# Sparse and stick-breaking attention on one Trainium2 core: value products cut along the keys instead of along the queries, one PSUM bank per head, each batch fed in two phases

## The chip, the cores and the metric

One kernel on one core of a Trainium2 chip. The metric is the device time of one execution in microseconds (us); lower is better. The engines are named as in the profile: PE is TensorE's matmul side, PEld its weight loads, DVE is VectorE, ACT is ScalarE, POOL is GpSimd, SP issues most of the DMAs.

## The reference, cut to what matters

The kernel computes a two-layer trunk over 2048 tokens. Two of its attention stages are touched. In the first layer it is stick-breaking attention with 8 heads of 64, strictly causal in blocks of 128 queries; in the second it is sparse attention with 16 heads of 64, where keys that were not chosen carry a very negative score in a table that is added. (The kernel multiplies the latents out to keys and values per head beforehand.)

```
# stick-breaking, one block of 128 queries, keys 0..L-1
z = einsum('bqhd,bkhd->bhqk', q, k) * scale
log_keep = where(causal, log_sigmoid(-z), 0)
suffix = cumsum(log_keep, reverse=True) - log_keep
a = where(causal, exp(log_sigmoid(z) + suffix), 0)
out = einsum('bhqk,bkhd->bqhd', a, v)          # the value product
# sparse, one block of 128 queries
s = einsum(q_lat, c_sel) * scale - slope * dist
p = softmax(where(sel_ok, s, -inf))
out = (p @ c_sel) @ w_uv                        # the value product
```

## The kernel before, in words

Both stages, `stick_breaking` (4 pairs of heads) and `sparse_attention` (8 pairs), have the same frame. Queries and keys come in blocks of 128. For one pair of heads, `paired_groups` (L1294) walks the 16 query blocks in the order of `TURNS` (L1290); for a block b the b+1 key blocks are cut into parts of at most four blocks, the last part first. One **group** is one part of one head: m key blocks, 1 to 4. The two heads of a pair alternate, so groups come in twos. A pair of heads has 80 groups, four groups make a **batch** (BATCH = 4); stick-breaking has 320 groups or 80 batches, sparse attention 640 groups or 160 batches. A **turn** is a set of query blocks whose results share one PSUM bank `o_ps`; there are 12 turns to a pair of heads.

What happens to a group, by engine:

- **score** (PE, `PairTiles.score`, L1367): three products in float32r, each with 64 rows (one head's 64 features; the pair's two heads lie in the two halves of the partitions) and a stationary of 128 queries, against up to 512 keys. The output goes to one of four banks (`s_ps` or `z_ps`).
- then in sparse attention **bias** on DVE (L1614, adds the table, takes the maximum) and the exponential on ACT (L1565); in stick-breaking the sigmoid on ACT (`keep`, L1824), the scan on DVE (L1872), the difference on POOL (L1851). In stick-breaking the sigmoid overwrites its bank, so the bank comes free with the scan.
- **turn** (PE, `turn_pair`, L1385): transposes of 64 query rows by 128 keys, stationary the 64x128 piece of the probabilities, moving a 64x64 identity; queries 0..63 of both heads go to bank `t_ps[0]`, queries 64..127 to `t_ps[1]`. The two pieces of a key block alternate between the two halves of the rows.
- **copy out** to `pT` in SBUF (stick-breaking: ACT, L1831; sparse: every fourth DVE, the others ACT, L1553).
- **feed** (PE, `feed_group`, L1396): the value product. Per key block and query half one matmul in plain float32, contraction over all 128 keys, stationary 128 keys x 64 queries, moving the values (64 columns, 65 in sparse attention with a column of ones), into the lower or upper 64 partitions of the turn's bank. The trace shows two instructions for each such matmul.
- at the end of a turn the **drain**: in sparse attention DVE divides (L1639, L1640) and POOL multiplies by the gate (L1590); in stick-breaking DVE multiplies by the gate, once per unit (L1884).

The order on PE is written out. In sparse attention one batch n is: turn(n), score(n+16), score(n+18), turn(n+2), then the four feeds of the batch before. In stick-breaking: turn(n), score(n+8), turn(n+2), score(n+10), then the four feeds of the batch before. Two banks `o_ps` alternate by turn, so the first feed of a turn waits for the drain of the turn before the last (L1523, L1796). DVE in sparse attention: one copy out, two biases, drains of turns that ended two batches earlier, two biases. In stick-breaking: two scans, such drains, two scans. `turn(n)` waits for the probabilities and for the copies of the two groups before; `score(k)` waits until the bank of group k-4 is free. SP loads the next pair's keys, queries, values and gates (`load_values` waits on `fed`).

Of the kernel before, what the change touches and what calls it, by code (L numbers as in the profile page):

```python
# [36 lines left out]
P = 128  # L37
# [1251 lines left out]

TURNS = [[0, 1], [2, 3], *([b] for b in range(NT - 1, 7, -1)), [7, 6], [5, 4]]  # L1290
BLOCKS = [b for turn in TURNS for b in turn]

def paired_groups(pairs):  # L1294

    units, out = [], []
    for j in range(pairs):  # L1300
        for turn, x, b in ((n, x, b) for n, turn in enumerate(TURNS) for x, b in enumerate(turn)):
            both = [Unit(j, hh, b, list(range(b + 1))) for hh in range(2)]
            parts = chunks(b + 1, GB)[::-1]
            for u in both:
                u.ng, u.turn, u.slot = len(parts), j * len(TURNS) + turn, 2 * (b - min(TURNS[turn])) + u.hh
# [89 lines left out]

def feed_group(nc, o_ps, pT, v, g, vc, fed, w=HD):  # L1396

    for x in range(g.m):
        for half in range(2):  # L1400
            x0 = (g.u.hh * g.m + x) * HD
            last = nc.tensor.matmul(o_ps[half * HD:(half + 1) * HD, 0:w], pT[half][:, x0:x0 + HD],  # L1402
                                    v[:, g.u.kbs[g.a + x], vc:vc + w],
                                    start=(g.first and x == 0 and g.u.hh == 0), stop=(g.last and x == g.m - 1),
                                    skip_group_check=True)
    last.then_inc(fed, 1)

def sparse_attention(nc, c, fm, kc, vc, gc, y, scores, ahead, tiles):
# [17 lines left out]
    with Scope(nc) as sc:  # L1427
# [25 lines left out]
        turned = sc.sem("turned")  # L1453
        taken = {"s": sc.sem("taken_s"), "v": sc.sem("taken_v")}
        fed = sc.sem("fed")
        slopes_set = sc.sem("slopes_set")
# [4 lines left out]
        with nc.Block() as block:  # L1461
# [37 lines left out]
            def _(pe):  # L1499
# [18 lines left out]

                def feed(n):
                    g = gs[n]  # L1520
                    u, p = g.u, g.u.j
                    if g.first and u.turn >= 2:
                        pe.wait_ge(drained, u.turn - 1)  # L1523
                    if n % (PER_PAIR) == 0:
                        pe.wait_ge(v_in[p % 2], (p // 2 + 1) * 32)
                        if n == 0:
                            pe.wait_ge(tables_set, 1)
                    if n % 2 == 0:
                        for x in (n, n + 1):
                            pe.wait_ge(taken[who[x]], nth[x])  # L1530
                    x0 = u.slot * SW
                    feed_group(nc, o_ps[u.turn % 2][:, x0:x0 + SW], [pT[(n - u.hh + x) % TB] for x in range(2)],
                               v[p % 2], g, SW * u.hh, fed, SW)
# [12 lines left out]
                for x in range(NG - BATCH, NG):  # L1546
                    feed(x)

            def copy_out(eng, copy, n):
                if n >= TB:  # L1550
                    eng.wait_ge(fed, n // 2 * 2 - TB + 2)
                eng.wait_ge(turned, n // 2 * 2 + 2)
                copy(pT[n % TB][:, 0:gs[n].m * P], t_ps[n % 2][:, 0:gs[n].m * P]).then_inc(taken[who[n]], 1)  # L1553

# [39 lines left out]
            def _(dve):  # L1594
# [38 lines left out]
                def drain(n):  # L1633
                    w = len(turns[n])
                    dve.wait_ge(fed, turns[n][0].turn_end + 1)
                    heads = o_ps[n % 2][:, 0:w * SW].rearrange("p (u w) -> p u w", w=SW)
                    if n >= 2:
                        dve.wait_ge(out_made, made_by[n - 2])
                    link(nc.vector.reciprocal(rden[:, n % 2, 0:w], heads[:, :, HD]))  # L1639
                    nc.vector.tensor_tensor(ob[n % 2][:, 0:w * HD].rearrange("p (u d) -> p u d", d=HD),  # L1640
                                            heads[:, :, 0:HD],
                                            rden[:, n % 2, 0:w].unsqueeze(2).broadcast_to([P, w, HD]), ALU.mult
                                            ).then_inc(drained, 1)
# [23 lines left out]
def stick_breaking(nc, c, fm, vals, gates, y_dram, ahead, tiles):  # L1667
# [11 lines left out]

    ends = [u.turn_end // BATCH for u in units]  # L1680
    freed_at = {part: 1 + max(u.end for u in units[:2 * NT] if u.b == part * GB) for part in (1, 2, 3)}
# [16 lines left out]
    with Scope(nc) as sc:  # L1698
# [5 lines left out]
        left = sc.sb("left", [P, CAP])  # L1704
        pT = [sc.sb(f"pT{k}", [P, BANK]) for k in range(TB)]
        z_ps = [sc.ps(f"z{k}", [P, BANK]) for k in range(4)]
        t_ps = [sc.ps(f"t{k}", [P, BANK]) for k in range(2)]
        o_ps = [sc.ps(f"o{k}", [P, BANK]) for k in range(2)]
        v_in = [ahead.v_in, sc.sem("v_in1")]
# [9 lines left out]
        turned = sc.sem("turned")  # L1719
        taken = sc.sem("taken")  # L1720
        fed = sc.sem("fed")
        out_made = sc.sem("out_made")

        with nc.Block() as block:
# [38 lines left out]
            def _(pe):  # L1763
# [27 lines left out]

                def feed(n):
                    g = gs[n]
                    u, p = g.u, g.u.j
                    if g.first and u.turn >= 2:
                        pe.wait_ge(out_made, made_by[u.turn - 2])  # L1796
                    if n % (PER_PAIR) == 0:
                        pe.wait_ge(v_in[p % 2], (p // 2 + 1) * 16)
                    if n % 2 == 0:
                        pe.wait_ge(taken, n + 2)  # L1800
                    x0 = u.slot * HD
                    feed_group(nc, o_ps[u.turn % 2][:, x0:x0 + HD], [pT[(n - u.hh + x) % TB] for x in range(2)], v[p % 2], g, HD * u.hh, fed)

                for k in range(0, LEAD, 2):
                    score(k)
                for n in range(0, NG, BATCH):
                    for a in range(n, n + BATCH, 2):
# [3 lines left out]
                    if n:  # L1811
                        for x in range(n - BATCH, n):
                            feed(x)
                for x in range(NG - BATCH, NG):
                    feed(x)

            @block.scalar
            def _(act):
# [8 lines left out]
                def copy_out(n):  # L1827
                    if n >= TB:
                        act.wait_ge(fed, n // 2 * 2 - TB + 2)
                    act.wait_ge(turned, n // 2 * 2 + 2)  # L1830
                    nc.scalar.copy(pT[n % TB][:, 0:gs[n].m * P], t_ps[n % 2][:, 0:gs[n].m * P]).then_inc(taken, 1)  # L1831

# [22 lines left out]
            def _(dve):  # L1855
# [19 lines left out]

                def output(ui):
                    u = units[ui]
                    p = u.j
                    if ui % (2 * NT) == 0:
                        dve.wait_ge(g_in[p % 2], (p // 2 + 1) * 16)  # L1880
                    dve.wait_ge(fed, u.turn_end + 1)
                    cc = slice(HD * u.hh, HD * u.hh + HD)
                    x0 = u.slot * HD
                    nc.vector.tensor_tensor(gt[p % 2][:, u.b, cc], o_ps[u.turn % 2][:, x0:x0 + HD],  # L1884
                                            gt[p % 2][:, u.b, cc], ALU.mult).then_inc(out_made, 1)

                def outputs(batch):
                    for ui, e in enumerate(ends):
                        if e == batch:
                            output(ui)  # L1890

# [1068 lines left out]
```

## Time and profile before

| | us |
|---|---|
| three runs | 3659.1, 3659.0, 3647.3 |
| median | 3659.0 |
| profiled execution, span from first to last instruction | 3662.1 |
| stick-breaking, first value product to last drain | 997 to 1386 |
| sparse attention, first score to last value product | 2720 to 3400 |
| PE busy over the whole span | 3333.1 |
| DVE busy | 2130.1 |
| ACT busy | 1898.0 |
| POOL busy | 815.7 |

The page shows no time of the profiled execution other than its span, which is 3.1 us above the median of the runs. Busy times of PE overlap at their ends, since a matmul is counted until its result has left the array; the time from one start to the next is what a matmul costs in a stream. The profile's granted clock is a share of full speed.

### The profile page before, as it was taken

How to read it: one execution, taken by the hardware profiler on the slowest of the kernel's cores; microseconds unless marked ns; L12 is line 12 of the kernel's file. 1: busy time of each engine (PE TensorE's matmuls, PEld its weight loads, DVE VectorE, ACT ScalarE, POOL GpSimd, SP SyncE). 2: the span in 40 equal slices, each digit the busy share in tenths (PEclk: the TensorE clock that was granted, in tenths of full speed). 3: DMA queues.
4: the chain of work that ended last, by engine and by line, in shares of the span. 5: the costliest groups of instructions: out<-in, count | busy, mean ns of one | idle time of the engine just before them, and what ended most of it. 6: DMA issues, size and time to landing. Idle time of an engine off the chain costs nothing. (4 is left out here: it accounts for less than half of the span.)

```text
span 3662.1 us, 90162 instructions
## 1 busy us (share of the span) xinstructions
PE 3333.1 (91%) x36876; PEld 2902.3 (79%) x36876; DVE 2130.1 (58%) x5023; ACT 1898.0 (52%) x3756; POOL 815.7 (22%) x900
## 2 busy tenths in 40 slices
PE   5899999989888888997797999997789999999899
PEld 5777899978777776885665898897678888888787
DVE  7100100028788893331199998996967777777322
ACT  5122211126677773221287766755468888888311
POOL 3222200001377770001101532521510000000000
PEclk9999999989899999998899999998899999999999
DMA  5333421159412314345421436335563333331432
GB/s 195 109 115 118 144 65 65 48 112 238 131 46 75 83 39 146 114 154 195 116 58 46 138 113 182 135 96 163 207 183 88 91 84 84 92 86 51 153 112 85
DMA packets 368257, 416.91 MB, mean 114 GB/s; under 512 B 51816, under 2 KB 272616, under 8 KB 366952
## 3 DMA queue, kind: packets, MB, share of 16 engines
q1 hardware_dynamic: 303096, 318.55, 30.1%
q10 hardware_dynamic: 64768, 92.81, 7.0%
q8 instruction: 283, 4.64, 0.5%
q14 instruction: 110, 0.90, 0.1%
HBM read 247.21 MB, written 164.10 MB: 112 GB/s over the span
## 5 line engine op out<-in xcount | busy, mean ns | idle before, releaser
L1402 PE MATMUL s_o<-s_v,s_pT 128*64 128x65 f32 (+1 forms) x13056 | 436.6, 224 | 9.6 <-issue 9.4
L1402 PEld LDWEIGHTS s_o<-s_v,s_pT 128*64 128x64 f32 x13056 | 402.0, 138 | 46.0 <-issue 24.6
L230 PE MATMUL s_acc<-s_wh,s_hT 128*128 128x256 f32 (+1 forms) x1408 | 430.6, 306 | 7.8 <-ACT s_parts L653 4.6
L232 PE MATMUL s_acc<-s_wh,s_hT 128*128 128x256 f32 (+1 forms) x1408 | 429.8, 305 | 0.0
L231 PE MATMUL s_acc<-s_wl,s_hT 128*128 128x256 f32 (+1 forms) x1408 | 429.7, 305 | 0.0
L230 PE MATMUL s_acc<-s_hT,s_wh 128*128 128x512 f32 x880 | 349.8, 397 | 57.3 <-DVE s_wl L329 25.8
L1565 ACT ACTIVATE s_probs<-s_probs,s_nmx 128x512 f32<-128x512 f32 (+3 forms) x640 | 388.8, 662 | 12.0 <-DVE s_nmx L1630 12.0
L1614 DVE CUSTOM_DVE_ANT_0 s_probs<-s_s,s_scores 128x512 f32<-128x512 f32 (+3 forms) x640 | 364.4, 607 | 8.9 <-issue 5.1
L2375 DVE TENSOR_SCALAR_CACHE_REDUCE s_scratch<-s_scores,s_thr 128x384 uint8<-128x384 f32 (+4 forms) x320 | 365.3, 1209 | 1.1
L231 PE MATMUL s_acc<-s_hT,s_wh 128*128 128x512 f32 x880 | 347.7, 395 | 0.0
L232 PE MATMUL s_acc<-s_hT,s_wl 128*128 128x512 f32 x880 | 347.5, 395 | 0.0
L326 DVE TENSOR_TENSOR s_gate<-s_ready 128x1 f32<-128x1 f32 x25 | 4.0, 159 | 572.3 <-PEq L383 378.4
L1851 POOL TENSOR_TENSOR s_share<-s_left 128x512 f32<-128x512 f32 (+4 forms) x320 | 290.4, 909 | 105.8 <-DVE s_left L1872 78.4
L2405 ACT ACTIVATE s_spare<-s_scores,s_thr 128x1664 f32<-128x1664 f32 (+6 forms) x142 | 249.7, 1759 | 113.2 <-DVE s_thr L2365 97.0
L1553 ACT COPY s_pT<-s_t 128x512 f32<-128x512 f32 (+2 forms) x480 | 239.3, 534 | 96.9 <-PE s_t L1392 92.0
L230 PEld LDWEIGHTS s_acc<-s_wh,s_hT 128*128 128x128 f32 x1408 | 266.2, 189 | 10.7 <-ACT s_parts L653 5.2
L313 POOL TENSOR_TENSOR s_parts<-s_parts 128x512 fp32r<-128x512 f32 x80 | 114.5, 1432 | 678.8 <-ACT s_parts L422 678.8
L232 PEld LDWEIGHTS s_acc<-s_wh,s_hT 128*128 128x128 f32 x1408 | 265.6, 189 | 0.0
L231 PEld LDWEIGHTS s_acc<-s_wl,s_hT 128*128 128x128 f32 x1408 | 264.4, 188 | 0.0
L2675 PE MATMUL s_o<-s_wh,s_yTh 128*128 128x512 f32 x640 | 255.0, 398 | 4.4 <-DVE s_wl L2740 4.4
L1872 DVE TENSOR_TENSOR_SCAN s_left<-s_z,s_left,s_ones 128x512 f32<-128x512 f32 x192 | 233.0, 1265 | 38.8 <-ACT s_z L1824 26.6
L2677 PE MATMUL s_o<-s_wh,s_yTl 128*128 128x512 f32 x640 | 250.5, 391 | 0.0
(278 smaller groups left out, 7180.2 us busy)
## 6 DMA issues: line engine op xcount, KB each, us to landing
fm<-s_parts ACTq DMA_DIRECT2D x120, 512.0 KB, 2.8
s_y<-y SPq DMA_DIRECT2D x32, 640.0 KB, 5.9
y<-s_g SPq DMA_DIRECT2D x18, 1024.0 KB, 5.8
kc<-s_parts SPq DMA_DIRECT2D x32, 512.0 KB, 3.3
s_w<-in_o_fm SPq DMA_DIRECT2D x25, 512.0 KB, 4.5
s_w<-in_o_w_in SPq DMA_DIRECT2D x12, 1024.0 KB, 5.6
s_qh<-fm SPq DMA_DIRECT2D x42, 256.0 KB, 3.2
s_ql<-fm SPq DMA_DIRECT2D x42, 256.0 KB, 3.7
```

Source lines behind the costliest of these rows:

```text
L230: nc.tensor.matmul(out, sh, mh, start=(j == 0), stop=False)
L231: nc.tensor.matmul(out, sh, ml, start=False, stop=False)
L232: ins = nc.tensor.matmul(out, sl, mh, start=False, stop=(j == n - 1))
L1402: last = nc.tensor.matmul(o_ps[half * HD:(half + 1) * HD, 0:w], pT[half][:, x0:x0 + HD], v[:, g.u.kbs[g.a + x], vc:vc + w], start=(g.first ...
L1553: copy(pT[n % TB][:, 0:gs[n].m * P], t_ps[n % 2][:, 0:gs[n].m * P]).then_inc(taken[who[n]], 1)
L1565: nc.scalar.activation(e, e, ACT.Exp, bias=nmx[:, us:us + 1], scale=slope[2 * u.j + u.hh]).then_inc(exp_made, 1)
L1614: nc.vector.tensor_tensor_reduce(out=probs[k % R][:, 0:g.m * P], in0=s_ps[k % 4][:, 0:g.m * P], in1=scores(u.b)[:, g.a * P:(g.a + g.m) * P ...
L1851: nc.gpsimd.tensor_tensor(share[k % R][:, 0:w], left[:, col[k] + 1:col[k] + 1 + w], left[:, col[k]:col[k] + w], ALU.subtract).then_inc(bro ...
L2375: v.tensor_scalar(self.junk[n % 2][:, 0:self.width(n)], self.scores(n + self.B0), self.thr[:, n:n + 1].bitcast(F32), None, ALU.is_ge, ALU.add,
L2405: self.nc.scalar.activation(signs[:, 0:self.width(n)], self.scores(n + self.B0), ACT.Sign, scale=-1.0, bias=self.thr[:, n:n + 1].bitcast(F32),
L2675: nc.tensor.matmul(o, th, mh, start=(j == 0), stop=False)
L2677: last = nc.tensor.matmul(o, tl, mh, start=False, stop=(j == KY - 1))
```

## The change

`feed_group` is replaced by `feed_half`. A value product now contracts over 64 keys only and covers all 128 queries: stationary 64 keys x 128 queries, moving 64 keys x 64 (65) values. To this end `pT` holds the two query halves of a key block side by side (`in_order`), so the copies out write blocks of 64 columns at a stride. The number of matmuls stays: four per key block and pair of heads. Each head has its own PSUM bank. In the first phase head 0 takes the lower 64 keys of each block and head 1 the upper 64, in the second phase the other way round; the second phase waits for the end of the first (`half_fed`), the next first phase for the end of the second (`fed`). Since both banks now belong to one turn, the first product of a turn waits for the drain of the turn directly before it. Turns must end with a batch, so blocks 11 to 8 are paired and a pair of heads has 10 turns instead of 12. PE's order becomes: turn, score, first phase, turn, score, second phase. In sparse attention DVE does the drain ahead of its copy out; in stick-breaking one multiplication drains a whole turn.

```diff
-TURNS = [[0, 1], [2, 3], *([b] for b in range(NT - 1, 7, -1)), [7, 6], [5, 4]]
+TURNS = [[0, 1], [2, 3], *([b] for b in range(NT - 1, 11, -1)), [11, 10], [9, 8], [7, 6], [5, 4]]
...
+                u.opens = b == TURNS[turn][0]
+                u.ng, u.turn, u.slot = len(parts), j * len(TURNS) + turn, b - min(TURNS[turn])
...
+def in_order(t, m):
+    return t[:, 0:2 * m * P].rearrange("p (x h q) -> p h x q", h=2, q=HD)
+
+def feed_half(nc, o_ps, pT, v, gs, SW, second):
+    m = gs[0].m
+    for x in range(m):
+        for g in gs:
+            half = (g.u.hh + 1) % 2 if second else g.u.hh
+            rows, x0 = slice(half * HD, (half + 1) * HD), (g.u.hh * m + x) * P
+            at = g.u.hh * BANK + g.u.slot * SW
+            last = nc.tensor.matmul(o_ps[:, at:at + SW], pT[rows, x0:x0 + P],
+                                    v[rows, g.u.kbs[g.a + x], g.u.hh * SW:(g.u.hh + 1) * SW],
+                                    start=(g.u.opens and g.first and not second and x == 0),
+                                    stop=(g.last and second and x == m - 1), skip_group_check=True)
+    return last
...
-        pT = [sc.sb(f"pT{k}", [P, BANK]) for k in range(TB)]
+        pT = [sc.sb(f"pT{k}", [P, 2 * BANK]) for k in range(TB // 2)]
...
-        o_ps = [sc.ps(f"o{k}", [P, BANK]) for k in range(2)]
+        o_ps = sc.ps("o", [P, 2 * BANK])
...
+                def first_halves(batch):
+                    if batch:
+                        pe.wait_ge(fed, batch)
+                    for n in range(batch, batch + BATCH, 2):
+                        u, p = gs[n].u, gs[n].u.j
+                        if gs[n].first and u.turn >= 1:
+                            pe.wait_ge(drained, u.turn)
...
+                        last = feed_half(nc, o_ps, pT[n % TB // 2], v[p % 2], gs[n:n + 2], SW, False)
+                    last.then_inc(half_fed, 1)
+
+                def second_halves(batch):
+                    pe.wait_ge(half_fed, batch // BATCH + 1)
+                    for n in range(batch, batch + BATCH, 2):
+                        feed_half(nc, o_ps, pT[n % TB // 2], v[gs[n].u.j % 2], gs[n:n + 2], SW, True).then_inc(fed, 2)
...
                     turn(n)
                     if n + LEAD < NG:
                         score(n + LEAD)
+                    if n:
+                        first_halves(n - BATCH)
+                    turn(n + 2)
+                    if n + LEAD < NG:
                         score(n + LEAD + 2)
-                    turn(n + 2)
                     if n:
-                        for x in range(n - BATCH, n):
-                            feed(x)
...
+                        second_halves(n - BATCH)
...
                 for n in range(0, NG, BATCH):
+                    outputs(n // BATCH - 2)
                     copy_out(dve, nc.vector.tensor_copy, n + 1)
                     bias(n + LEAD)
                     bias(n + LEAD + 1)
-                    outputs(n // BATCH - 2)
...
+                def output(n):
+                    turn = turns[n]
+                    p, b, w = turn[0].j, min(u.b for u in turn), len(turn) // 2
...
+                    own = gt[p % 2][:, b:b + w, :].rearrange("p b (h d) -> p h b d", h=2)
+                    heads = o_ps[:].rearrange("p (h c) -> p h c", h=2)[:, :, 0:w * HD].rearrange(
+                        "p h (b d) -> p h b d", d=HD)
+                    nc.vector.tensor_tensor(own, heads, own, ALU.mult).then_inc(out_made, len(turn))
```

## Rows read from the trace of the kernel before

**Rows 1.** The page, part 1: busy us (share of the span) xinstructions.
```profile
PE 3333.1 (91%) x36876; PEld 2902.3 (79%) x36876; DVE 2130.1 (58%) x5023; ACT 1898.0 (52%) x3756; POOL 815.7 (22%) x900
```

**Rows 2.** Busy times in two stretches: PE, PEld, DVE, ACT, POOL, granted clock, DMA.
```profile
997.00:1387.00 390.00, 342.44 (x7636) 283.71 (x7634) 337.65 (x435) 279.09 (x618) 282.30 (x426) 1.00 0.21 58
2738.00:3401.00 663.00, 640.75 (x14814) 574.93 (x14812) 508.07 (x2412) 569.41 (x1099) 52.15 (x95) 1.00 0.29 80
```

**Rows 3.** Waits in stick-breaking: who for whom, us in total, times, longest.
```profile
PE s_t L1392 <- ACT s_pT L1831: 28.7, 48, 0.9
DVE s_left L1872 <- ACT s_z L1824: 28.4, 40, 1.5
DVE s_left L1872 <- POOL s_share L1851: 15.8, 15, 1.3
```

**Rows 4.** Timeline of PE, one full batch of sparse attention: start us, us, what.
```profile
2747.05 2.09 PE L1402 MATMUL s_o<-s_v,s_pT 128*64 128x65 f32 x64
2749.07 0.71 PE L1392 MATMUL s_t<-s_ident,s_probs 64*128 64x64 f32 x16
2749.59 0.48 PE L1374 MATMUL s_s<-s_kh,s_qh 64*128 64x512 f32 x2
2749.91 0.40 PE L1374 MATMUL s_s<-s_kh,s_ql 64*128 64x512 f32 x2
2750.14 0.40 PE L1374 MATMUL s_s<-s_kl,s_qh 64*128 64x512 f32 x2
...
2751.07 0.65 PE L1392 MATMUL s_t<-s_ident,s_probs 64*128 64x64 f32 x16
2751.65 1.56 PE L1402 MATMUL s_o<-s_v,s_pT 128*64 128x65 f32 x46
```

**Rows 5.** Timeline of the weight loads from 2744.9 us on.
```profile
2745.43 0.20 PEld L1374 LDWEIGHTS s_s<-s_kh,s_ql 64*128 64x128 f32 x2
...
2745.77 0.19 PEld L1374 LDWEIGHTS s_s<-s_kh,s_ql 64*128 64x128 f32 x2
...
2747.05 1.95 PEld L1402 LDWEIGHTS s_o<-s_v,s_pT 128*64 128x64 f32 x64
2749.07 0.57 PEld L1392 LDWEIGHTS s_t<-s_ident,s_probs 64*128 64x128 f32 x16
2749.56 0.20 PEld L1374 LDWEIGHTS s_s<-s_kh,s_qh 64*128 64x128 f32 x2
2749.68 0.19 PEld L1374 LDWEIGHTS s_s<-s_kh,s_ql 64*128 64x128 f32 x2
```

**Rows 6.** Single instructions by line: count, duration ns min/median/max, first and last start.
```profile
L1402 PEld LDWEIGHTS s_o<-s_v,s_pT x13056: 132/138/227, 996.8 to 3400.4; 128*64 128x64 f32 x198
L1402 PE MATMUL s_o<-s_v,s_pT x13056: 217/222/367, 996.8 to 3400.4; 128*64 128x65 f32 x132, 128*64 128x64 f32 x66
...
L1392 PEld LDWEIGHTS s_t<-s_ident,s_probs x4352: 133/138/143, 2728.5 to 3397.6; 64*128 64x128 f32 x198
...
L1374 PEld LDWEIGHTS s_s<-s_kh,s_ql x512: 182/188/336, 2719.8 to 3381.2; 64*128 64x128 f32 x171
```

**Rows 7.** Timeline of a stick-breaking batch: ACT's copies and sigmoids, PE, DVE's scans.
```profile
1149.78 1.07 ACT L1831 COPY s_pT<-s_t 128x512 f32<-128x512 f32 x2 [1.59 <-PE s_t L1392]
...
1150.73 1.09 ACT L1824 ACTIVATE s_z<-s_z 128x512 f32<-128x512 f32 x2
...
1150.99 0.71 PE L1392 MATMUL s_t<-s_ident,s_share 64*128 64x64 f32 x16 [0.56 <-ACT s_pT L1831]
...
1151.47 2.46 DVE L1872 TENSOR_TENSOR_SCAN s_left<-s_z,s_left,s_ones 128x512 f32<-128x512 f32 x2 [1.18 <-POOL s_share L1851]
```

**Rows 8.** Timeline of DVE around a drain in sparse attention.
```profile
3005.63 0.69 DVE L1614 CUSTOM_DVE_ANT_0 s_probs<-s_s,s_scores 128x512 f32<-128x512 f32 x1
...
3006.24 0.17 DVE L1639 RECIPROCAL s_rden<-s_o 128x2 f32<-128x2 f32 x1
3006.44 0.29 DVE L1640 TENSOR_TENSOR s_ob<-s_o,s_rden 128x128 f32<-128x128 f32 x1
```

More of the change, by code:

```diff
@@ L1300, in paired_groups @@
     for j in range(pairs):
-        for turn, x, b in ((n, x, b) for n, turn in enumerate(TURNS) for x, b in enumerate(turn)):
+        for turn, b in ((n, b) for n, turn in enumerate(TURNS) for b in turn):
             both = [Unit(j, hh, b, list(range(b + 1))) for hh in range(2)]
@@ L1304, in paired_groups @@
             for u in both:
-                u.ng, u.turn, u.slot = len(parts), j * len(TURNS) + turn, 2 * (b - min(TURNS[turn])) + u.hh
+                u.opens = b == TURNS[turn][0]
+                u.ng, u.turn, u.slot = len(parts), j * len(TURNS) + turn, b - min(TURNS[turn])
             for n, (a, m) in enumerate(parts):
@@ L1393, in turn_pair @@
     last.then_inc(turned, 2)
[L1396 to L1406, printed above, removed]
+def in_order(t, m):
[12 more added lines that the diff above has]
+    return last
 def sparse_attention(nc, c, fm, kc, vc, gc, y, scores, ahead, tiles):
@@ L1454, in sparse_attention @@
         taken = {"s": sc.sem("taken_s"), "v": sc.sem("taken_v")}
+        half_fed = sc.sem("half_fed")
         fed = sc.sem("fed")
@@ L1517, in turn @@
                     turn_pair(nc, c, t_ps, [probs[x % R] for x in (n, n + 1)], gs[n:n + 2], turned)
[L1519 to L1528, printed above, removed]
+                def first_halves(batch):
[5 more added lines that the diff above has]
+                            pe.wait_ge(drained, u.turn)
+                        if n % (PER_PAIR) == 0:
+                            pe.wait_ge(v_in[p % 2], (p // 2 + 1) * 32)
+                            if n == 0:
+                                pe.wait_ge(tables_set, 1)
                         for x in (n, n + 1):
                             pe.wait_ge(taken[who[x]], nth[x])
-                    x0 = u.slot * SW
-                    feed_group(nc, o_ps[u.turn % 2][:, x0:x0 + SW], [pT[(n - u.hh + x) % TB] for x in range(2)],
-                               v[p % 2], g, SW * u.hh, fed, SW)
+                        last = feed_half(nc, o_ps, pT[n % TB // 2], v[p % 2], gs[n:n + 2], SW, False)
[4 more added lines that the diff above has]
+                        feed_half(nc, o_ps, pT[n % TB // 2], v[gs[n].u.j % 2], gs[n:n + 2], SW, True).then_inc(fed, 2)
                 for k in range(0, LEAD, 2):
@@ L1540, in _ @@
                         score(n + LEAD)
+                    if n:
+                        first_halves(n - BATCH)
+                    turn(n + 2)
+                    if n + LEAD < NG:
                         score(n + LEAD + 2)
-                    turn(n + 2)
                     if n:
-                        for x in range(n - BATCH, n):
-                            feed(x)
-                for x in range(NG - BATCH, NG):
-                    feed(x)
+                        second_halves(n - BATCH)
+                first_halves(NG - BATCH)
+                second_halves(NG - BATCH)
             def copy_out(eng, copy, n):
@@ L1678, in stick_breaking @@
     assert PER_PAIR % BATCH == 0
-    ends = [u.turn_end // BATCH for u in units]
+    turns = [[u for u in units if u.turn == n] for n in range(units[-1].turn + 1)]
+    ends = [turn[0].turn_end // BATCH for turn in turns]
     freed_at = {part: 1 + max(u.end for u in units[:2 * NT] if u.b == part * GB) for part in (1, 2, 3)}
@@ L1704, in stick_breaking @@
         left = sc.sb("left", [P, CAP])
-        pT = [sc.sb(f"pT{k}", [P, BANK]) for k in range(TB)]
+        pT = [sc.sb(f"pT{k}", [P, 2 * BANK]) for k in range(TB // 2)]
         z_ps = [sc.ps(f"z{k}", [P, BANK]) for k in range(4)]
         t_ps = [sc.ps(f"t{k}", [P, BANK]) for k in range(2)]
-        o_ps = [sc.ps(f"o{k}", [P, BANK]) for k in range(2)]
+        o_ps = sc.ps("o", [P, 2 * BANK])
         v_in = [ahead.v_in, sc.sem("v_in1")]
@@ L1720, in stick_breaking @@
         taken = sc.sem("taken")
+        half_fed = sc.sem("half_fed")
         fed = sc.sem("fed")
@@ L1790, in turn, with first_halves, second_halves @@
                     turn_pair(nc, c, t_ps, [share[x % R] for x in (n, n + 1)], gs[n:n + 2], turned)
[L1792 to L1799, printed above, removed]
-                        pe.wait_ge(taken, n + 2)
-                    x0 = u.slot * HD
-                    feed_group(nc, o_ps[u.turn % 2][:, x0:x0 + HD], [pT[(n - u.hh + x) % TB] for x in range(2)], v[p % 2], g, HD * u.hh, fed)
+                def first_halves(batch):
+                    if batch:
+                        pe.wait_ge(fed, batch)
+                    for n in range(batch, batch + BATCH, 2):
+                        u, p = gs[n].u, gs[n].u.j
+                        if gs[n].first and u.turn >= 1:
+                            pe.wait_ge(out_made, made_by[u.turn - 1])
+                        if n % (PER_PAIR) == 0:
+                            pe.wait_ge(v_in[p % 2], (p // 2 + 1) * 16)
+                        pe.wait_ge(taken, n + 2)
+                        last = feed_half(nc, o_ps, pT[n % TB // 2], v[p % 2], gs[n:n + 2], HD, False)
+                    last.then_inc(half_fed, 1)
+                def second_halves(batch):
+                    pe.wait_ge(half_fed, batch // BATCH + 1)
+                    for n in range(batch, batch + BATCH, 2):
+                        feed_half(nc, o_ps, pT[n % TB // 2], v[gs[n].u.j % 2], gs[n:n + 2], HD, True).then_inc(fed, 2)
                 for k in range(0, LEAD, 2):
@@ L1806, in _ @@
                 for n in range(0, NG, BATCH):
-                    for a in range(n, n + BATCH, 2):
+                    for a, halves in ((n, first_halves), (n + 2, second_halves)):
                         turn(a)
@@ L1810, in _ @@
                             score(a + LEAD)
[L1811 to L1815, printed above, removed]
+                        if n:
+                            halves(n - BATCH)
+                first_halves(NG - BATCH)
+                second_halves(NG - BATCH)
             @block.scalar
@@ L1830, in copy_out @@
                     act.wait_ge(turned, n // 2 * 2 + 2)
-                    nc.scalar.copy(pT[n % TB][:, 0:gs[n].m * P], t_ps[n % 2][:, 0:gs[n].m * P]).then_inc(taken, 1)
+                    nc.scalar.copy(in_order(pT[n % TB // 2], gs[n].m)[:, n % 2, :, :],
+                                   t_ps[n % 2][:, 0:gs[n].m * P].rearrange("p (x q) -> p x q", q=HD)
+                                   ).then_inc(taken, 1)
                 for k in range(LEAD):
```

32 lines of the change are left out of this document (14 added, 18 removed).

## The prediction

> **What bounds the kernel now.** I read the page first: PE is busy 91% of the span [rows 1]. That is an average, so I read the two touched stages by their windows. Stick-breaking has no saturated engine; its waits go round a ring: PE for ACT's copies (28.7 us), DVE for ACT's sigmoid (28.4) and for POOL (15.8) [rows 3]. A microsecond more on PE costs one in sparse attention; in stick-breaking it costs one once the slack is used up.
>
> Then the PE timeline of one full batch (all parts of four key blocks), in starts [rows 4]: value products 2747.05, transposes 2749.07, first score 2749.59, next transposes 2751.07, next value products 2751.65: 4.60 us. Three things are to be seen. First, 64 value instructions fill 2.02 us; their loads come 64 in 1.95 us [rows 5], so two every (1.95 - 0.14)/31 = 0.0584 us. Second, a matmul here lasts 0.22 us [rows 6], so the last value product began at 2747.05 + 2.09 - 0.22 = 2748.92 and the transposes only 0.15 us later; the last transpose began at 2751.07 + 0.65 - 0.22 = 2751.50, the value products again 0.15 later. From transposes to scores, both in 64-row pieces, it is 2749.59 - (2749.07 + 0.71 - 0.22) = 0.03 us. Going to 128 rows x 64 columns and back costs 0.12 us each time. Third, the first product of a score run is followed after 0.32 us by the second, those after by 0.23 or 0.24.
>
> **The change, part by part.**
>
> *The cut switches go.* Two per batch, 0.24 us. Sparse: 160 batches x 0.24 = 38 us gained. In stick-breaking, where 80 x 0.24 = 19 us go, it counts within PE's sum below. What is late next: the same PE stream.
>
> *One more start of a score run.* Scores now come in two runs per batch, each after transposes, whose loads can't be hidden behind a 0.22 us matmul: 0.32 - 0.235 = 0.085 us more, x 160 = 14 us in sparse attention [rows 4].
>
> *The value products themselves.* Their number stays at 13056 instructions, 6528 twos. What changes is the load: 64 columns before, 128 now. No row shows a plain float32 load of 64 rows x 128 columns, so I bound it.
> The nearest rows are the score loads: 64 rows x 128 columns, plain matmuls, two at a time in the two row halves. A pair of them starts at 2749.56 and the next at 2749.68, 0.12 us later, although the products behind them have 512 columns and run on; in a run of short scores they come at 2745.43 and, three pairs on, at 2745.77, 0.113 us per pair [rows 5]. The shortest durations agree: 182 ns with 128 columns, 132 ns with the value products' 64 columns [rows 6]; the fixed part is the same and 64 further columns cost 50 ns. So 64 columns take some 55 ns, which is why two old ones come every 58 ns, and 128 columns some 110 ns.
> The other end is the transposes: also 128 columns, but 133 ns at least [rows 6] and 16 in 0.57 us, (0.57 - 0.14)/7 = 0.062 us per two [rows 5]. They are not plain products; they pass data through. In duration the old value load equals theirs with half the columns, so it loads columns at the score load's pace. I take 0.113 us; ends 0.062 and, if a row half could not load during its own product, 0.113 + 0.058 = 0.171.
> Added: 6528 x (0.113 - 0.0584) = 356 us of PE time, 238 in sparse attention and 119 in stick-breaking.
>
> The Trainium skill ("TensorE: Matmul & The Clock Gate", LDWEIGHTS) says that a load's time goes by columns over 1.2, so 53 ns for 64 and 107 ns for 128 whatever the rows; by that the addition would be 6528 x (0.107 - 0.0584) = 317 us. The score rows agree (110 to 120 ns), the transposes' 62 ns per two loads do not, so the rule is not general in this trace.
>
> *One drain sooner.* The first value product of a turn now waits for the drain of the turn just before; behind it on PE wait transposes, scores and the second phase. Sparse: PE reaches it 0.52 (transposes) + 0.79 (score) = 1.31 us after the last second phase. DVE has two biases of some 0.62 us to finish, but with a second phase of 32/2 x 0.113 = 1.8 us they are done before it ends; the drain is 0.17 + 0.29 us [rows 8], up to 0.6 for two blocks. Cost 0; if the products stay short, about 0.15 us x 80 turns = 12 us.
> Stick-breaking: the drain stands behind two scans. The score they need began 2.6 us before the end of the second phase; ACT first makes two copies, 1.07 us, then one sigmoid, 0.55 us; scans of 2.46 us [rows 7] therefore end about 1.8 us after it, the drain at 2.1. PE waits 0.8 us, 4 pairs x 10 turns = 40 times: 32 us. Ends 0 and, if the scans lag by one, 60.
>
> *Copies out, buffers, drains, queues.* The copies have as many elements in runs of 64 columns: 0. They stand behind transposes that now come later, and have until the next value phase: covered. Fewer, wider drains relieve DVE and POOL, which don't bound: 0. SP's loads of values wait on `fed` as before and have a whole pair of heads ahead. The waits on `half_fed` and `fed` are met while transposes and a score (1.3 us) run: 0.
>
> *The sum.* Sparse: 238 - 38 + 14 = +214 us. Stick-breaking, PE per batch now: 27.2 twos x 0.058 = 1.59, transposes 27.2 x 0.033 = 0.89, scores 2 x 0.79 x 0.87 (parts average 3.4 of 4) = 1.37, switches 0.24: 4.1 of 390/80 = 4.88 us. After: 4.1 - 0.24 + 0.09 + 27.2 x 0.0546 = 5.44; DVE's share, 338/80 = 4.2, is below it, so PE sets the pace: 80 x 5.44 + 32 = 467 us, +77. Together +291 us. The profiled execution is 3.1 us above the median of 3659.0; from the median: **3950 us**. Its own range: load 0.107 to 0.120 per two (-39, +46) and the stick-breaking wait 0 to 60: 3880 to 4020.
>
> **Rivals.**
>
> *Loads as fast as the transposes'.* 0.062 instead of 0.113: 6528 x 0.0036 = +23 us, of which 16 sparse. Sparse 16 - 38 + 14 + 12 = +4. In stick-breaking the half feed between the two transposes hides ACT's copies (28.7 us on PE), evens the score times, but at each turn DVE's next scan comes later by about 0.8 us x 40 = 32: about 0. Time 3663. For it: the same shape of load exists at 62 ns; against: equal duration for half the columns.
>
> *Faster: the even rhythm wins.* Place: PE between the score and the second transposes of a batch. The price of a two stays at 0.0584, sparse gains 38 - 14 = 24, and in stick-breaking the 28 us that DVE waits for the sigmoid go, with the drains hidden: 3659 - 52 = 3607. It decides only where a two costs under 0.0584 + (52 - 18)/6528 = 0.064 us; above that nothing here pays for the products.
>
> *Worse: no overlap within a row half.* 0.171 per two: 6528 x 0.113 = 735, less 24 and the slack of stick-breaking (58): about 4310. Against: a score pair's loads come while the products before them still run.
>
> *The switches stay* (the gap is something else, such as the wait instruction): +38 in sparse, within the range.
>
> **How the numbers follow.** Load-bound as summed 0.72; worse 0.04; loads like the transposes' 0.12; faster 0.12. The likeliest range, 3880 to 4020, holds some 0.65; to leave out no more than 0.2 I go down to 3610, through the second case and into the third. 0.5% is 18 us, about what a measurement can tell: slower 0.76, same 0.12, faster 0.12.
>
> **What would show it.** In the profile after: value loads with 128 columns of about 185 ns (138 now), 32 value instructions in about 1.8 us instead of 0.93; gaps of 0.03 us between value products and transposes; sparse attention from 680 to some 890 us with PE busy throughout and ACT and DVE idler; stick-breaking about 465 us, PE waiting for L1884's successor once a turn. The forecast is wrong if value loads last about 138 ns; then 32 instructions take about 1.0 us and the stages keep their length. The step most at risk is the price of one load.

## The result, and the profile after

| | before | after |
|---|---|---|
| median of 4 runs, us | 3655.2 | 3928.6 (3921.0 to 3944.4) |
| profiled execution, span | 3662.1 | 3942.6 |
| stick-breaking | 997 to 1386 | 994 to 1509 |
| sparse attention | 2720 to 3401 | 2838 to 3681 |

The ratio is 1.076, with a 95% interval of 1.074 to 1.078: slower by 273 us. Outside the two stages nothing moved by more than 5 us: up to 994 (before 997), between them 1329 us (before 1334), behind them 261 and 261.

The page of the changed kernel, part 1, and the two groups of the value products in part 5:

```profile
PE 3637.1 (92%) x36876; PEld 3296.2 (84%) x36876; DVE 2141.1 (54%) x4903; ACT 1911.9 (48%) x3756; POOL 813.4 (21%) x884
...
L1413 PEld LDWEIGHTS s_o<-s_v,s_pT 64*128 64x128 f32 x13056 | 851.7, 196 | 71.9 <-issue 60.6
L1413 PE MATMUL s_o<-s_v,s_pT 64*128 64x65 f32 (+1 forms) x13056 | 845.2, 278 | 45.3 <-issue 45.1
```

As many instructions as before on PE [rows 1], but 304 us more of busy time, and 394 us more on the loads. DVE has 120 instructions fewer and as much to do.

The two stages by windows (PE, PEld, DVE, ACT, POOL, granted clock, DMA share, GB/s):

```profile
994.00:1509.00 515.00, 477.84 (x7660) 456.66 (x7656) 338.71 (x348) 284.52 (x622) 284.75 (x428) 0.88 0.16 44
...
2838.00:3681.00 843.00, 831.74 (x14976) 811.74 (x14976) 536.63 (x2467) 590.73 (x1120) 49.68 (x95) 1.00 0.25 67
```

Sparse attention is 162 us longer and PE idle for 11 of its 843 us; before it was idle for 25 of 681 (the 663 us of [rows 2] leave out the first 18). Stick-breaking is 126 us longer, and there two things show beside the products: the granted clock is 0.88 (1.00 before), and PE idles 37 us although DVE is busy for only two thirds of the stage.

PE in a full half batch of sparse attention, beside [rows 4] (start us, us, what), then its loads, beside [rows 5]:

```profile
2862.77 1.93 PE L1413 MATMUL s_o<-s_v,s_pT 64*128 64x65 f32 x32
2864.50 0.66 PE L1393 MATMUL s_t<-s_ident,s_probs 64*128 64x64 f32 x15
2864.97 0.48 PE L1375 MATMUL s_s<-s_kh,s_qh 64*128 64x512 f32 x1
...
2865.75 1.94 PE L1413 MATMUL s_o<-s_v,s_pT 64*128 64x65 f32 x32
```

```profile
L1413 PEld LDWEIGHTS s_o<-s_v,s_pT x8704: 182/188/194, 2852.1 to 3680.5; 64*128 64x128 f32 x198
```

32 value instructions take 1.93 us from the first start to the last end and one lasts 0.27, so a two (two instructions side by side) comes every (1.93 - 0.27)/15 = 0.111 us; the load lasts 182 ns at the least, the score loads' figure [rows 6], and no longer 132. The gap ahead of the transposes is gone (2862.77 + 1.93 - 0.27 = 2864.43, transposes at 2864.50). A half batch takes 2.98 us, a batch 5.96, where it was 4.60. The forecast column adds the prediction's terms (+1.75 for 32 twos, -0.12 for each switch, +0.085 for the score start) to the column of before:

| one full batch, us | before | forecast | after |
|---|---|---|---|
| value products and what follows them | 2.02 | 3.65 | 3.46 |
| two transposes | 1.10 | 0.98 | 0.94 |
| two scores | 1.48 | 1.56 | 1.56 |
| sum | 4.60 | 6.19 | 5.96 |

Stick-breaking at the border of a turn (timeline of all engines):

```profile
1142.94 0.43 PE L1375 MATMUL s_z<-s_kl,s_qh 64*128 64x512 f32 x2
...
1143.79 0.27 DVE L1916 TENSOR_TENSOR s_g<-s_o,s_g 128x128 f32<-128x128 f32 x1
1144.12 1.67 PEld L1413 LDWEIGHTS s_o<-s_v,s_pT 64*128 64x128 f32 x28 [1.20 <-issue]
1144.15 1.78 PE L1413 MATMUL s_o<-s_v,s_pT 64*128 64x64 f32 x28 [0.79 <-issue]
```

PE has done its score and stands still until DVE, after two scans, has drained the last turn's bank. The waits of the stage hold such pauses (who for whom, us in total, times, longest):

```profile
PE s_o L1413 <- issue: 35.2, 36, 2.0
```

And the granted clock over the stage, in stretches of 50 us:

```profile
1044.00:1094.00 50.00, 45.93 (x844) 44.40 (x841) 38.58 (x40) 31.52 (x70) 32.78 (x51) 0.99 0.08 23
...
1194.00:1244.00 50.00, 47.77 (x713) 45.88 (x712) 29.88 (x32) 25.48 (x59) 24.29 (x45) 0.80 0.15 44
...
1444.00:1494.00 50.00, 47.78 (x673) 46.62 (x672) 27.51 (x28) 22.72 (x51) 23.26 (x36) 0.74 0.03 7
```

At 0.80 and 0.74 PE is busier than at 0.99 and executes fewer matmuls: 713 and 673 in 50 us, not 844. Part of the stage ran at the lower level of 1.2 GHz. One such fall, in PE's timeline: a pause of 1.38 us in front of the drain, the next 32 products still at their pace, the 32 after them at half of it.

```profile
1217.16 2.00 PE L1413 MATMUL s_o<-s_v,s_pT 64*128 64x64 f32 x32 [1.38 <-issue]
...
1220.91 3.56 PE L1413 MATMUL s_o<-s_v,s_pT 64*128 64x64 f32 x32
```

The stage has nine falls like it (not counting its first 16 us), each within about 3 us of the end of a pause of 1.06 to 1.61 us; other pauses of that length, and one of 1.98, are followed by none.

### The profile page after: what moved, and what is told of

It reads as the page before. It is cut to its first block and busy times, and to the rows that moved or that the text cites. A ratio compares the mean times of both kernels' runs of the same rounds, so it can differ in the third digit from the quotient of the medians.

```text
span 3942.6 us, 90156 instructions
## 1 busy us (share of the span) xinstructions
PE 3637.1 (92%) x36876; PEld 3296.2 (84%) x36876; DVE 2141.1 (54%) x4903; ACT 1911.9 (48%) x3756; POOL 813.4 (21%) x884
## 5 line engine op out<-in xcount | busy, mean ns | idle before, releaser
L1413 PEld LDWEIGHTS s_o<-s_v,s_pT 64*128 64x128 f32 x13056 | 851.7, 196 | 71.9 <-issue 60.6
L1413 PE MATMUL s_o<-s_v,s_pT 64*128 64x65 f32 (+1 forms) x13056 | 845.2, 278 | 45.3 <-issue 45.1
L1860 ACT COPY s_pT<-s_t 128x512 f32<-128x512 f32 (+3 forms) x320 | 151.4, 525 | 213.5 <-PE s_t L1393 213.0
```

The lines of the kernel that those rows point to most:

```text
L1413: last = nc.tensor.matmul(o_ps[:, at:at + SW], pT[rows, x0:x0 + P], v[rows, g.u.kbs[g.a + x], g.u.hh * SW:(g.u.hh + 1) * SW], start=(g.u.o ...
```

## The experiments

The theory: the products' pace is that of their weight loads, and a load costs by its columns (128 instead of 64). In stick-breaking the late drain adds pauses, and the loss of clock comes on top of it. The rivals: the number of rows or the side by side of two row halves sets the pace; the moving side sets it; the two phases cost by themselves.

### Whole arrays: 128 rows x 128 columns

```
# feed_half, called once per batch, after both scores
-            half = (g.u.hh + 1) % 2 if second else g.u.hh
-            rows, x0 = slice(half * HD, (half + 1) * HD), (g.u.hh * m + x) * P
+            rows, x0 = slice(0, P), (g.u.hh * m + x) * P
```

> The changed kernel, but each key block of a head is one product over all 128 keys and all 128 queries, in one phase at the end of a batch: half as many value instructions (6528), none of them in row halves. Theory 'load': a plain float32 load of 128 columns takes 0.11 us wherever it stands, and whole-array loads come one at a time, so 6528 x 0.11 = 718 us, the same PE time as the 6528 twos of the changed kernel; the two cut switches of a batch (0.24 us) come back. Sparse attention (first score to last value product) 860 to 885 us instead of 843, the whole 3880 to 3980. Rival 'row halves': the price lies in two row halves working side by side or in the two phases; then a whole product costs what a two cost before, 0.06 us, and the whole comes to 3600 to 3700.

Measured: 4046.4 us, ratio 1.108 (1.104 to 1.113). PE in sparse attention, and the loads:

```profile
2999.97 3.79 PE L1412 MATMUL s_o<-s_v,s_pT 128*128 128x65 f32 x32
...
3005.35 0.59 PE L1393 MATMUL s_t<-s_ident,s_probs 64*128 64x64 f32 x12 [0.19 <-DVE s_pT L1561]
```

```profile
L1412 PEld LDWEIGHTS s_o<-s_v,s_pT x4352: 186/192/192, 2827.5 to 3770.4; 128*128 128x128 f32 x198
```

One whole-array instruction every (3.79 - 0.27)/31 = 0.1135 us, half as many of them: the pace of two row halves side by side (0.111). Neither the rows nor the cutting into halves matter, the 128 columns do. The total is 66 us above the range that was expected. Sparse attention took 960 us, 117 more than in the changed kernel, where 17 to 42 more were expected. PE was idle for 46 of them instead of 11: with the products in one lump, the second transposes of a batch wait for DVE's copy:

```profile
PE s_t L1393 <- DVE s_pT L1561: 42.3, 107, 1.1
```

The other 82 us are busy time; the two cut switches that come back account for 38 of them, the rest was not taken apart.

### Half the columns: 64 rows x 64 columns

```
-            last = nc.tensor.matmul(o_ps[:, at:at + SW], pT[rows, x0:x0 + P],
+            q0 = half * HD
+            last = nc.tensor.matmul(o_ps[q0:q0 + HD, at:at + SW], pT[rows, x0 + q0:x0 + q0 + HD],
```

> The changed kernel with the same number of value instructions, the same row halves, phases, banks and waits, but with 64 stationary columns instead of 128: each phase feeds only the query half that has the number of its key half, so half of the value products are left out. Theory 'load': two such instructions come every 0.058 us instead of 0.110, load durations fall from 188 to about 138 ns, PE loses 6528 x 0.052 = 340 us; less is gained where another engine or a cut switch (0.12 us each, up to four a batch) sets the pace: the whole 3590 to 3720. Rival 'row halves' (the price lies in the halves, the phases or the banks): as the changed kernel, 3900 to 3950.

Measured: 3739.5 us, ratio 1.024 (1.022 to 1.026). PE and the loads of sparse attention:

```profile
2857.65 0.71 PE L1393 MATMUL s_t<-s_ident,s_probs 64*128 64x64 f32 x16
...
2859.04 1.15 PE L1414 MATMUL s_o<-s_v,s_pT 64*64 64x65 f32 x32
2860.12 0.59 PE L1393 MATMUL s_t<-s_ident,s_probs 64*128 64x64 f32 x12
```

```profile
L1414 PEld LDWEIGHTS s_o<-s_v,s_pT x8704: 129/135/228, 2756.7 to 3478.0; 64*64 64x64 f32 x198
```

Half the columns, half the time: two every (1.15 - 0.22)/15 = 0.062 us. The total is 20 us above the range. In sparse attention (736 us, 681 before) the gaps came back: from the last value product's start, 2859.04 + 1.15 - 0.22 = 2859.97, to the transposes 0.15 us. A piece of 64 x 64 is again another cut than the transposes' 64 x 128, so what costs is a change of the cut, in rows or in columns. Stick-breaking took 422 us, 33 more than before with loads of the same pace; there PE waits for the late drain:

```profile
PE s_o L1414 <- issue: 55.0, 38, 2.0
```

### The drain ahead of the scans

Why did stick-breaking lose 126 us and not 77? The changed kernel with one call moved, in DVE's loop of stick-breaking:

```
+                    outputs(n // BATCH - 2)
                     scan(n + SCAN_LEAD)
                     scan(n + SCAN_LEAD + 1)
-                    outputs(n // BATCH - 2)
```

> The changed kernel; in stick-breaking DVE does the drain ahead of the two scans instead of behind them. Theory: the drain of a turn stands behind two scans, so PE waits 0.8 to 2 us at 37 to 40 turns, 45 us in all, and in those pauses the granted clock falls (0.88 over the stage, 1.00 before). With the drain first PE waits under 0.5 us a turn: stick-breaking from 515 to about 480 us with the clock as it is, to 420 to 450 if the clock comes back; the whole 3840 to 3900. Rival: the pauses come from the scans' own lateness; then the stage keeps its 515 us and the whole its 3929.

Measured: 3846.5 us, ratio 1.0535 (1.0515 to 1.0555). One stretch (the clock is 1.00 in all of them), the products of the stage with their first and last start, and DVE's new wait:

```profile
1144.00:1194.00 50.00, 49.83 (x940) 47.42 (x934) 38.95 (x42) 33.02 (x75) 34.34 (x56) 1.00 0.15 44
```

```profile
L1413 PE MATMUL s_o<-s_v,s_pT x4352: 213/272/345, 992.4 to 1415.3; 64*128 64x64 f32 x198
```

```profile
DVE s_g L1916 <- PE s_o L1413: 58.8, 30, 2.9
```

The stage falls from 515 to 424 us. PE's busy time, 478 us in the changed kernel, is 419 here with the same instructions; its idle time falls from 37 to 5. So of 91 us, 32 were pauses and 59 the lower clock that came with them in this kernel. DVE now waits 59 us for PE in front of the drain, out of its slack.

The pauses alone don't set that loss. With half the columns the same late drain made more of them (55.0 us, above, most of them 1.0 to 2.0 us long), and the clock of that stage was 0.98: it fell five times, each time at the end of such a pause or right behind it, and was back within 8 us, where in the changed kernel it stayed low for up to 20, and from the last fall to the end of the stage. With whole arrays PE was idle for 40 of 494 us, never more than 0.9 at once, and the clock was 1.00.

### Half the moving side

The changed kernel with the early drain; in stick-breaking alone each product moves half of the value columns, and half of every output's sums is left out:

```
+            c0, c1 = (0, SW) if SW > HD else (HD // 2, HD) if half == 0 else (0, HD // 2)
-            last = nc.tensor.matmul(o_ps[:, at:at + SW], pT[rows, x0:x0 + P], v[rows, ..., g.u.hh * SW:(g.u.hh + 1) * SW],
+            last = nc.tensor.matmul(o_ps[:, at + c0:at + c1], pT[rows, x0:x0 + P], v[rows, ..., g.u.hh * SW + c0:g.u.hh * SW + c1],
```

> The changed kernel with the stick-breaking drain ahead of the scans (so that the stage runs at a granted clock of 1.00, 424 us long), and in stick-breaking alone each value product moves only half of the value columns: the pieces of the first row half give columns 32 to 63 of an output, those of the second row half columns 0 to 31, so half of each output's sums is left out there. Each weight load stays 64 rows x 128 columns, the moving side falls from 64 to 32 columns a product. If the loads set the rate, as the prediction had it, two products still take 0.110 us, the stage stays at 415 to 430 us and the total at 3835 to 3860 us. If the moving side sets it, two take 0.055 to 0.065 us, which over 52 pairs a batch x 40 batches x 0.050 us is about 100 us of TensorE time: TensorE's busy time in the stage falls from 419 to about 320 us and the stage to the 340 to 370 us that VectorE's 339 us busy allow, total 3760 to 3790 us.

Measured: 4153.5 us (4124.0 to 4192.4), ratio 1.140 (1.134 to 1.146), far outside both. Windows of the stage (columns as above), then PE early in it and late in it:

```profile
1044.00:1094.00 50.00, 49.88 (x930) 47.48 (x926) 38.91 (x42) 32.96 (x75) 34.40 (x57) 0.99 0.15 45
1094.00:1144.00 50.00, 50.00 (x494) 46.41 (x492) 26.19 (x27) 21.47 (x47) 21.41 (x34) 0.50 0.33 86
```

```profile
1056.22 1.87 PE L1414 MATMUL s_o<-s_v,s_pT 64*128 64x32 f32 x32
...
1434.15 3.46 PE L1414 MATMUL s_o<-s_v,s_pT 64*128 64x32 f32 x32
```

For the first 100 us the clock is 0.97 and 0.99, and there the question is answered: 32 products with half the moving columns take 1.87 us, two every (1.87 - 0.23)/15 = 0.109. The moving side doesn't set the pace; the loads do. (The changed kernel executed 935 matmuls in the same 50 us with the early drain, this one 930.) Then the clock fell to 0.50, the lower level, and stayed there for the rest of the stage. No pause went ahead of it: PE was idle for 0.1 us from 1044 to 1094 and not at all from 1094 to 1644; the products took 3.46 us, and the stage 690 us (999 to 1689). Neither theory had that.

### The two phases alone

The kernel before, whole value products, in stick-breaking two groups after each score:

```
-                    if n:
-                        for x in range(n - BATCH, n):
-                            feed(x)
+                        if n:
+                            for x in range(a - BATCH, a - BATCH + 2):
+                                feed(x)
```

> The kernel before, only PE's order in stick-breaking changed to that of the changed kernel: turn, score, two feeds, turn, score, two feeds; the old cut with 64 columns stays. Theory 'rhythm': PE's 28.7 us of waits for ACT's copies and DVE's 28.4 us for the sigmoid go; PE has 80 x 0.33 = 26 us of further switches and score starts, which fit into its slack: stick-breaking from 389 to 360 to 375 us, the whole 14 to 30 us faster. Rival: the ring over POOL and the scans sets the pace or the further switches eat the gain: no difference, or up to 10 us slower.

Measured: 3627.5 us, ratio 0.9947 (0.9928 to 0.9967): faster than both kernels. The stage took 369 us; of its waits:

```profile
PEld s_o L1402 <- ACT s_pT L1831: 22.4, 61, 0.4
DVE s_left L1872 <- ACT s_z L1824: 22.0, 35, 1.3
...
DVE s_left L1872 <- POOL s_share L1851: 4.1, 11, 0.6
...
PE s_t L1392 <- ACT s_pT L1831: 1.6, 9, 0.2
```

PE's wait for ACT's copies at the transposes falls from 28.7 to 1.6 us, DVE's for the sigmoid from 28.4 to 22.0, and its wait for POOL from 15.8 to 4.1 [rows 3]. What stands in their place is smaller: the value products' loads wait 22.4 us for the copies (9.2 before), never over 0.4 at once.

Is it the cover or the rhythm? All four groups between the two scores:

```
                         turn(a)
                         if a + LEAD < NG:
                             score(a + LEAD)
-                    if n:
-                        for x in range(n - BATCH, n):
-                            feed(x)
+                        if n and a == n:
+                            for x in range(n - BATCH, n):
+                                feed(x)
```

> The kernel before, with one edit in TensorE's order of the stick-breaking stage: a batch runs turn, score, all four groups' products, turn, score, instead of turn, score, turn, score, products. So it has no more changes between 64-row and 128-row work than before, and it separates two readings of the run with two products after each score. If that run's gain of 20 us in the stage came from the drain and the copies having more cover (products standing between the two transposes), this one should gain as much or more: one cut less to pay twice, 0.24 us x 40 turns = 10 us, so a stick-breaking stage of 355 to 372 us (before 389) and 3625 to 3645 us in all. If it came from the even rhythm (half of the products after each score), this one should keep most of the waits for the copies, at the second score's end, and give a stage of 375 to 392 us and 3645 to 3660 us.

Measured: 3662.0 us, ratio 1.002 (1.000 to 1.003). The stage's products, and two waits from 1005 to 1350 us:

```profile
L1402 PE MATMUL s_o<-s_v,s_pT x4352: 221/222/368, 993.7 to 1392.9; 128*64 128x64 f32 x198
```

```profile
PEld s_t L1392 <- POOL s_share L1851: 43.6, 48, 1.0
...
PE s_t L1392 <- ACT s_pT L1831: 27.4, 47, 0.9
```

Some 399 us: none of the gain, a little worse even than the 375 to 392 expected. PE's wait for the copies at the transposes is no smaller than before (24.9 us in the same stretch): it has only moved to the other transposes, those with no products in front. What pays is that products stand in front of every one of them.

And the same two phases in sparse attention as well:

```
                     turn(n)
                     if n + LEAD < NG:
                         score(n + LEAD)
-                        score(n + LEAD + 2)
+                    if n:
+                        for x in range(n - BATCH, n - BATCH + 2):
+                            feed(x)
                     turn(n + 2)
+                    if n + LEAD < NG:
+                        score(n + LEAD + 2)
                     if n:
-                        for x in range(n - BATCH, n):
+                        for x in range(n - BATCH + 2, n):
                             feed(x)
```

> The kernel before, with whole 128x128 value products, but in two phases of two groups in both stages (turn, score, products of two groups, turn, score, products of the other two). It is the 'two phases' part of the change alone, without the 64-row pieces. The stick-breaking stage should come out as in the run with the two phases there alone (369 us). In the sparse stage each of the 160 batches gets one more pair of cuts into and out of whole-array work (0.24 us) and one more start of a score run (0.085 us): 0.33 x 160 = 52 us, which takes the stage from 681 to about 733 us and the total to 3627 + 52 = 3680 us (3660 to 3700). If the phases hide as much as they cost (the rival of an even rhythm), the sparse stage stays at 675 to 700 us and the total at 3620 to 3645 us.

Measured: 3665.8 us, ratio 1.003 (1.002 to 1.004). Its products in sparse attention, first and last start; in the run with the two phases in stick-breaking alone they went from 2700.4 to 3363.6:

```profile
L1402 PE MATMUL s_o<-s_v,s_pT x8704: 217/222/272, 2703.6 to 3405.8; 128*64 128x65 f32 x198
```

702 us instead of 663: +39, and the total is 38 above that run's. Two phases of whole products cost in sparse attention about what was expected of the added cuts and score starts (52 us, 0.33 a batch). A full batch is two of these halves, 4.96 us instead of 4.60:

```profile
2742.82 0.71 PE L1392 MATMUL s_t<-s_ident,s_probs 64*128 64x64 f32 x16
...
2745.30 0.71 PE L1392 MATMUL s_t<-s_ident,s_probs 64*128 64x64 f32 x16
```

PE's busy time grew by 47 us and its idle time fell by 9, which gives 38 of the 39. This is the price that pieces cut like the scores avoid; it is about a sixth of what they pay there in loads, 4352 x 0.0526 = 229 us.

### Two phases and the early drain together

```
# on top of the two phases in stick-breaking alone, DVE
+                    outputs(n // BATCH - 2)
                     scan(n + SCAN_LEAD)
                     scan(n + SCAN_LEAD + 1)
-                    outputs(n // BATCH - 2)
```

> The kernel before with two phases in stick-breaking alone (the version that ran 19 us faster than before), and VectorE's drain put ahead of its two scans there. In that version TensorE still waits 12 us for what the profile calls issue at the first product of a turn (33 times), and no edge of the granted clock is lost (1.00). If the early drain takes these waits away and the later scans cost nothing, the stage falls from 369 to about 357 us and the total from 3627 to 3615 us. The rival: before a drain can run, VectorE has to wait for the end of the turn's last product, and the scans behind it now wait too; in the changed kernel this wait was 59 us and was paid out of VectorE's slack (339 busy of 424 us), but here the slack is only 30 us (339 of 369), so the stage grows to 375 to 400 us and the total to 3633 to 3660 us.

Measured: 3637.0 us, ratio 0.995 (0.994 to 0.996), the same as without the early drain within the intervals. The products went from 992.8 to 1368.4, 376 us instead of 369, the lower edge of what the rival expected. Two waits from 1005 to 1350 us show why:

```profile
DVE s_g L1884 <- PE s_o L1402: 18.2, 21, 1.4
...
PEld s_o L1402 <- issue: 13.1, 36, 0.4
```

The wait that was to go (12 us) is still there, and DVE now waits 18 us for the turn's last product, a wait that it had without the early drain for 4.4 us in the whole stage. The edit that is worth 82 us in the changed kernel is worth nothing here, where the clock was whole.

## Why the prediction was right

3950 us was forecast (3610 to 4020), 3928.6 measured, by the mechanism with 0.72 of the chance. Against the median of before in the same comparison (3655.2) it is +273 us, forecast +291. The closeness is partly luck: sparse attention came 52 us below its sum, stick-breaking 49 above, and the two errors cancel.

- **The load** (0.113 us per two, ends 0.062 and 0.171): 0.111 measured. That it goes by columns is shown by four cuts: 0.0584 (128 x 64) and 0.062 (64 x 64) per two for 64 columns, 0.111 per two (64 x 128) and 0.1135 per single whole array (128 x 128) for 128, and that it is the load and not the moving side by the products of half width. The Trainium skill's rule ("TensorE: Matmul & The Clock Gate", LDWEIGHTS, columns over 1.2) gives 107 ns and was about as near as the score rows: by it the estimate is +317 us instead of +356, by the measured pace 6528 x 0.0526 = +343.
- **The cut switches** (-38 in sparse attention): the gap ahead of the transposes went; it came back with 64 x 64 pieces, and 160 more pairs of cuts with one more score start each cost 39 us, net of 9 us less idle time. Shown.
- **One more score start** (+14): two scores take 1.56 instead of 1.48 us a batch, 0.08 (0.085 forecast).
- **Sparse attention** (+214, measured +162): by the sum a full batch takes 6.19 us, and it took 5.96: 3.46 instead of 3.65 for the value products, 0.94 instead of 0.98 for the transposes. These 0.23 us, on batches 0.85 full on average, are an estimated 0.20 x 160 = 31 us. The sum also left before's idle time of PE standing; it fell from 25 to 11 us. Together 45 of the 52.
- **The stick-breaking stage without the wait** (5.44 x 80 = 435): 424 measured, with the drain early.
- **The late drain** (0.8 us, 40 times, 32 us): 36 waits, 35.2 us. In place and size as forecast. The printed steps don't add up to the scans' end at 1.8 us behind the second phase (-2.6 + 1.07 + 0.55 + 2.46 = 1.5), but 1.8 is what happened: in the border row above the scans ended at 1143.87, the phase at 1142.11.
- **The step that failed** is that nothing else came of this wait. The sum took the clock of before, 1.00, for granted; it fell to 0.88, which added 59 us of busy time. The wait was priced by its length alone. In this kernel moving the drain took both the pauses and the drop away; the half-column and half-value runs show that pauses are not the whole cause.
- **Rivals.** "Loads as the transposes'" fell with the first load row. "The even rhythm wins" has its mechanism: two phases are worth 20 us in stick-breaking (28 and more were forecast), but its condition, a two under 0.064 us, isn't met by 128-column loads. "No overlap" (0.171) fell.

Still open: why the transposes, with 128 columns too, keep 0.062 us per two, and what exactly in the stage's work lets the clock fall, and come back soon or late; the runs show only when it does. The pieces along the keys have no version here that saves their loads: the early drain leaves them 194 us behind the kernel before. The best kernel is the one with whole products and two phases in stick-breaking alone.

## What to carry to other kernels

When a plain matmul's moving side is short, cost it by the columns of its stationary side: a cut along the contraction that widens the stationary from 64 to 128 columns doubles the price of every product here, whatever it saves in switches. Spreading work evenly between its dependents can be had without a new cut, by moving calls; try that alone first. And when a new wait lands on TensorE, read the granted clock of the stage and not only the wait: taking 32 us of pauses away gave back 91 here. The factor is this kernel's; with half the columns 55 us of pauses left the clock at 0.98.

## What was not expected of the hardware

- The granted clock of a stage with loads as its bound is fragile here. Before, PE was busy 342 of 390 us in stick-breaking at 1.00 [rows 2]; with 128-column loads it was busy 478 of 515 at 0.88; with the moving side halved too, PE had no pause and the clock fell to 0.50 after 100 us. The busy share of the profile doesn't tell it.
- Products that move fewer columns can thus be slower: the stage took 690 us with half the columns moved, 424 with all. At 0.50 two loads side by side took (3.46 - 0.40)/15 = 0.204 us, against 0.109 at the full clock, so the loads go by this clock as well.
- A change of the cut costs in either direction: 128 x 64 to 64 x 128 and 64 x 64 to 64 x 128 both show a 0.15 us gap, against 0.07 between products and transposes of one cut (2864.43 to 2864.50).
